# A two-layer encoder with expert retrieval: U ring of seven slots, V split at column 1024

## The reference

```python
def peer_ffn(xn, w_query, sub_keys, u, v):
    b, s, d = xn.shape
    K = PEER_TOPK
    q = (xn @ w_query).reshape(b, s, PEER_HEADS, 2, PEER_DKEY // 2)
    sc = jnp.einsum('bshpc,hpnc->bshpn', q, sub_keys).astype(jnp.float32)
    s_top, i_top = lax.top_k(sc, K)
    ...
    best, pos = lax.top_k(cand, K)
    expert = jnp.take_along_axis(cand_idx, pos, axis=-1)
    gate = jax.nn.softmax(best, axis=-1).astype(xn.dtype)
    ...
        act = jax.nn.gelu(jnp.einsum('tkd,td->tk', u[e], xt), approximate=False)
        return jnp.einsum('tk,tkd->td', g * act, v[e])
```

## Time and profile before

| what | us |
|---|---|
| median of 3 runs | 3390.19 (3378.97 to 3415.09) |
| the profiled execution | 3391.91, its span 3390.0 |
| DVE busy | 2366.2 (70%) |
| PE busy | 1921.9 (57%) |
| POOL busy | 1631.4 (48%) |
| data moved | 1067.07 MB, 315 GB/s over the span |

### The profile page before, as it was taken

One profiled execution on the slowest core, in us unless ns is written; L12 is line 12 of the kernel. 1 busy time (PEld: TensorE's weight loads), 2 busy tenths in 40 slices (PEclk: granted clock), 3 DMA queues, 4 the chain that ended last, 5 costly groups with the idle time before them and its releaser, 6 DMA issues.

```text
span 3390.0 us, 19864 instructions
## 1 busy us (share of the span) xinstructions
PE 1921.9 (57%) x6432; PEld 1415.5 (42%) x6432; DVE 2366.2 (70%) x3291; ACT 525.3 (15%) x1373; POOL 1631.4 (48%) x1028
## 2 busy tenths in 40 slices
PE   8999994714003300599999366322024105899992
PEld 4684543613003300467777245311023004677772
DVE  1340217889888887966666759889888889756668
ACT  1331200000009900100000000000079201000000
POOL 0000003355568877454444413546688878744445
PEclk9999997967555555589999688766555555799996
DMA  5334256787789999789999957877899998899998
GB/s 215 132 117 149 75 203 267 305 307 297 293 322 385 388 363 362 246 305 409 410 410 409 390 217 303 313 293 298 310 368 391 394 384 279 292 410 410 409 409 352
DMA packets 194502, 1067.07 MB, mean 315 GB/s; under 512 B 21856, under 2 KB 22240, under 8 KB 121312
## 3 DMA queue, kind: packets, MB, share of 16 engines
q0 software_dynamic: 147456, 822.15, 63.3%
q1 hardware_dynamic: 46944, 243.67, 18.2%
HBM read 1063.63 MB, written 2.10 MB: 314 GB/s over the span
## 4 chain that ended last, share of the span: by engine, by line
DMA 35%; DVE 21%; POOL 21%; PE 16%; issue 6%; ACT 0%; DVEq 0%; SPq 0%; POOLq 0%
DMA xnT<-pvg,idx_all 21%; POOL arena L392 16%; DMA arena<-pu,idx_all 13%; DVE arena L1012 8%; PE bank L1169 6%; DVE h L1031 3%; PE bank L1254 3%; POOL xnT L405 3%; POOL arena L405 3%; PE bank L1363 2%; PE bank L1410 1%; PE bank L1374 1%; DVE gB L1046 1%; PE bank L1432 1%; DVE gB L1042 1%
## 5 line engine op out<-in xcount | busy, mean ns | idle before, releaser
L392 POOL DMA_INDIRECT arena<-pu,idx_all x512 | 1056.0, 2063 | 1197.5 <-DVE idx_all L992 608.2
L1012 DVE CUSTOM_DVE_ANT_0 arena<-arena 128x2048 f32<-128x2048 f32 x512 | 1168.3, 2291 | 242.0 <-DMA arena<-pu,idx_all 239.3
L1459 PE MATMUL bank<-arena 128*128 128x480 f32 x2048 | 829.9, 569 | 2.0 <-ACT arena L651 1.4
L1459 PEld LDWEIGHTS bank<-arena 128*128 128x128 f32 x2048 | 605.0, 296 | 226.1 <-issue 4.9
L1031 DVE SCALAR_TENSOR_TENSOR h<-arena,cst,h 128x1088 f32<-128x1088 f32 x290 | 391.2, 1351 | 178.1 <-DMA arena<-pvg,idx_all 177.9
L405 POOL DMA_INDIRECT arena<-pvg,idx_all x290 | 313.9, 1082 | 305.8 <-DVE h L1031 271.7
L1031 DVE SCALAR_TENSOR_TENSOR h<-xnT,cst,h 128x1088 f32<-128x1088 f32 x222 | 299.7, 1351 | 140.9 <-DMA xnT<-pvg,idx_all 140.7
L405 POOL DMA_INDIRECT xnT<-pvg,idx_all x222 | 261.3, 1177 | 234.4 <-DVE h L1031 212.1
L1440 PE MATMUL bank<-cst,arena 128*128 128x128 f32 x8 | 2.8, 447 | 629.0 <-DVE cst L1018 629.0
L1440 PEld LDWEIGHTS bank<-cst,arena 128*128 128x128 f32 x8 | 1.2, 204 | 630.2 <-DVE cst L1018 630.2
L1410 PE MATMUL bank<-xnT,arena 128*128 128x256 f32 (+1 forms) x1280 | 244.7, 356 | 16.9 <-DMA arena<-wq 13.3
(11 more groups left out here) (193 smaller groups left out, 1630.8 us busy)
## 6 DMA issues: line engine op xcount, KB each, us to landing
arena<-pvd SPq DMA_DIRECT2D x256, 480.0 KB, 6.8
arena<-w_proj SPq DMA_DIRECT2D x22, 2048.0 KB, 8.2
arena<-wq SPq DMA_DIRECT2D x16, 2048.0 KB, 12.2
arena<-w_out SPq DMA_DIRECT2D x9, 2048.0 KB, 8.3
arena<-pu,idx_all POOLq DMA_INDIRECT x512, 7.8
gB<-gains SPq DMA_DIRECT2D x5, 1024.0 KB, 10.2
arena<-pvg,idx_all POOLq DMA_INDIRECT x290, 13.4
arena<-pool_w SPq DMA_DIRECT2D x1, 4096.0 KB, 14.3
```

Of the source, the lines that this page charges most:

```text
L392: nc.gpsimd.indirect_dma_start(U[:, n % UR], None, pu[L], bass.IndirectOffsetOnAxis(idx_all[:, g, k:k + 1], 0)).then_inc(u_got[n % UR], 16)
L1012: vec.tensor_tensor_reduce(out=u, in0=u, in1=xns[t], scale=1.0, scalar=0.0, op0=ALU.mult, op1=ALU.add, accum_out=act[:, t, hk:hk + 1]).the ...
L1459: ins = mm(psum[2 * t + c][:, 0:VH], W[t][:, :, n], vdense[:, n % DR, c * VH:(c + 1) * VH], start=n == 0, stop=n == NK - 1)
```

## The change

The U ring has seven slots in place of four. Slots 0 to 3 stay, the fifth is 2048 columns behind the one-hot tiles (arena 37248, over the third output weight slice of layer 0), the sixth and seventh depend on the block: for block 0 they lie at 12288 (over another output weight slice), for block 1 at 24576, over the keys and the routing scratch. Gathers 0 to 3 of layer 0 now wait for the first output projection, gathers 4 to 6 for all eight; gather 128 also waits until scores and expert numbers of all heads are done; every later gather waits for the dot seven before it, in place of four. V is split at column 1024: 1024 columns gathered (before 1088) and 1024 in the dense product (before 960, so matmuls of 512 columns in place of 480). The V ring has eight slots of 1024 in place of seven of 1088, four of them in xnT; the dense ring starts at 4096. Dots still read both operands from SBUF.

```diff
--- before.py
+++ after.py
@@ -52,17 +52,17 @@
 HALF = KC // 2
 
 WR = 3
-UR = 4
-VD, VG = 960, D - 960
+UR = 7
+VD, VG = 1024, D - 1024
 VH = VD // 2
-VR, DR = 7, 4
+VR, DR = 8, 4
 HK = PH * PK
 GROUPS = TB * PH
 ROWS = GROUPS * PK
 EVENTS = PH + 2
 QT = 4
 QUADS = P // QT
-W_AT, V_AT, VD_AT, T_AT = 8192, 0, 4352, 40960
+W_AT, V_AT, VD_AT, T_AT = 8192, 0, 4096, 40960
 POOLW = (2, 4, 8, 16)
 ARENA = 41344
 OUT_AT = 33152
@@ -116,7 +116,6 @@
             return carve
 
 
-        U = carver(0, ARENA)(UR, D)
         W = [carver(W_AT + t * P * P, ARENA)(P, P) for t in range(TB)]
         wqb2 = carver(W_AT, ARENA)(KC, 2 * P)
         wqb = carver(W_AT + 2 * KC * P * 2, ARENA)(2, KC, 2 * P)
@@ -135,6 +134,14 @@
         xn1 = carve(D)
         oh1 = carve(2, QT, P)
         oh2 = carve(2, QT, P)
+        fifth = carve(D)
+
+        def ring(at, n):
+
+            return [arena[:, at + i * D:at + (i + 1) * D] for i in range(n)]
+
+        shared = ring(0, 4) + [fifth]
+        U = [shared + ring(W_AT + KC * S, 2), shared + ring(W_AT + P * P, 2)]
         sT = carver(T_AT, ARENA)(3, P)
         wq_slots = [wqb[:, 0], wqb[:, 1], wqb2]
         xns = [xn0, xn1]
@@ -158,13 +165,13 @@
         exs, exr = spare(TB), spare(TB)
 
         xnT_flat = xnT[:, :, :].rearrange("p k s -> p (k s)")
-        vslots = [xnT_flat[:, i * VG:(i + 1) * VG] for i in range(3)]
-        vslots += [arena[:, V_AT + i * VG:V_AT + (i + 1) * VG] for i in range(VR - 3)]
+        vslots = [xnT_flat[:, i * VG:(i + 1) * VG] for i in range(4)]
+        vslots += [arena[:, V_AT + i * VG:V_AT + (i + 1) * VG] for i in range(VR - 4)]
         vdense = carver(VD_AT, W_AT)(DR, VD)
         goh1 = gB[:, 0:2 * QT * P].rearrange("p (b i n) -> p b i n", b=2, i=QT)
         goh2 = gB[:, 2 * QT * P:4 * QT * P].rearrange("p (b i n) -> p b i n", b=2, i=QT)
 
-        poolw = U.rearrange("p a b -> p (a b)").rearrange("p (g k c) -> p g k c", g=4, k=4)
+        poolw = carver(0, W_AT)(4, 4, BANK)
         slot1 = wqb[:, 1].rearrange("p k c -> p (k c)")
         PM = slot1[:, 0:D].rearrange("p (g t s) -> p g t s", g=4, t=TB)
         lsB = slot1[:, D:2 * D]
@@ -386,11 +393,17 @@
                 if n >= UR:
                     pool.wait_ge(s["dot_done"], L * ROWS + n - UR + 1)
                 elif L:
-                    pool.wait_ge(s["py_mm"], 4 + n + 1)
+                    pool.wait_ge(s["py_mm"], 4 + min(n, 3) + 1)
+                else:
+                    pool.wait_ge(s["out_mm"], TB * NO if n >= 4 else 1)
+                if n == HK:
+
+                    pool.wait_ge(s["sc_done"], (L + 1) * EVENTS)
+                    pool.wait_ge(s["idx_ready"], (L + 1) * EVENTS)
                 if k == 0:
                     pool.wait_ge(s["idx_ready"], L * EVENTS + event(g // PH, g % PH) + 1)
                 nc.gpsimd.indirect_dma_start(
-                    U[:, n % UR], None, pu[L], bass.IndirectOffsetOnAxis(idx_all[:, g, k:k + 1], 0)
+                    U[n // HK][n % UR], None, pu[L], bass.IndirectOffsetOnAxis(idx_all[:, g, k:k + 1], 0)
                 ).then_inc(u_got[n % UR], 16)
 
             def gather_v(L, m):
@@ -398,7 +411,7 @@
                 t, hk = m % TB, m // TB
                 if m >= VR:
                     pool.wait_ge(s["vacc_done"], L * ROWS + m - VR + 1)
-                elif m >= 3:
+                elif m >= 4:
                     pool.wait_ge(s["dot_done"], (L + 1) * ROWS)
                 else:
                     pool.wait_ge(s["q_mm"], (L + 1) * EVENTS)
@@ -1004,11 +1017,14 @@
                                        ex[:, tsl], exr[:, tsl].unsqueeze(2).to_broadcast([P, nt, PK]), ALU.mult))
 
 
+            ucount = [0] * UR
+
             def dot(L, n):
 
                 t, hk = n // HK, n % HK
-                v.wait_ge(u_got[n % UR], L * 16 * ROWS // UR + landed(n, UR))
-                u = U[:, n % UR]
+                ucount[n % UR] += 1
+                v.wait_ge(u_got[n % UR], 16 * ucount[n % UR])
+                u = U[t][n % UR]
                 vec.tensor_tensor_reduce(out=u, in0=u, in1=xns[t], scale=1.0, scalar=0.0, op0=ALU.mult, op1=ALU.add,
                                          accum_out=act[:, t, hk:hk + 1]).then_inc(s["dot_done"], 1)
 
```

## The result

The changed kernel takes 3215.3 us (median of 4, 3214.4 to 3215.6) against 3397.2 us (median of 4, 3379.0 to 3415.1) of the kernel before, run beside it: ratio 0.946, 95% interval 0.941 to 0.952. The profiled execution took 3215.5 us, 176.4 us less than that of before; the forecast was 187 less.

A forecast was written before the change was run, and what follows sets the result against it. The prediction held the four U slots, not bandwidth, for the bound of the 150 dots behind routing. Layer terms of -98 and -89 us took the profiled 3391.9 us to 3205 us; range 3168 to 3290, its terms' own ends 3176 and 3278.

The forecast's parts named there:

- The main step: 150 dots behind routing: four slots, not bandwidth, bind; 2.84 us a dot falls to 2.48 if the queue never runs dry.
- (b): Stage of 150 dots with nothing else on DVE, 946 to 1371 us in layer 0: forecast -60 and -46 us.
- six rows landed ahead: At dot 106, start of (b): six rows counted as landed, so 144 more must land; 365 us at 2.52 us each.
- (a): Stage of 74 dots beside routing, 668 to 946 us in layer 0: waits fall to 5 us, -34 and -30 us.
- Start of layer 0: First 32 dots: gathers 4 to 6 wait for all eight output projections, dot 4 starts near 551 us; +4 us.
- Layer 1: Start of layer 1: gathers 0 to 6 go at once, taking 5 of 8.1 us of waits off; -5 us.
- V: V split at 1024: shorter adds and gathers, dense matmuls 443 us with some ten adds behind; -8 us a layer.
- (c) and (d): One-hot tiles with V adds, then dense matmuls with the tail of adds: together -8 us a layer, from -10 to 0.
- The sum: Layer 0 -98 us, layer 1 -89 us: 3391.9 - 187 = 3205 us; forecast as summed given chance 0.70.
- Full DMA engines: First rival: transfers already full in (b), so a longer queue gains nothing there; 3311 us, chance 0.11.
- PE at the end: Second rival: PE sets the end of the dense part, +23 us a layer instead of -8; 3267 us, chance 0.13.
- POOL shut out by dots: Third rival: a full ring of seven blocks POOL's gathers, 3.33 us a dot in (b); 3539 us, chance 0.04.

The follow-up runs named there:

- the half dots with seven slots: The changed kernel, but each dot covers only the first 1024 of the 2048 columns, gathers staying whole: 3097.4 us (one run).
- routing three dots earlier: Changed kernel with layer 0's first slot order and V-add waits mended, plus each head's three routing pieces three dots earlier: 3187.6 us, ratio 0.938 to the kernel before.
- the ring alone: The kernel before with only the U ring raised to seven slots, V still split at 960: 3231.5 us, ratio 0.952.
- the half dots with four slots: U ring of four, V split at 1024, each dot over 1024 columns only, same bytes gathered: 3159.7 us (one run).
- the V part alone: The kernel before with only V split at 1024 and a V ring of eight, U ring of four: 3381.8 us, ratio 0.996.
- the half gathers: The changed kernel, but each U gather brings only 1024 columns while dots still run over 2048: 3144.8 us (one run).

## Why the prediction was right

**The main step held.** In (b) the four-slot ring and not the bandwidth was the bound, and with seven slots the landings follow each other at 2.5 us. Forecast -60 and -46 us, measured -55.8 and -42.7. It was reckoned from one paced run of three dots; the half dots with seven slots (367.2 us) and with four (371.9 us) show both halves of the claim.

**What was mis-sized in it** was "six rows landed ahead". Five rows lay ready at dot 106 (the gathers 106 to 110), number 111 landed 0.3 us into the stage, and number 112 could not be issued before 918.5 us. Its row landed at 926.3 us, 8.0 us into the stage; the other 143 followed at 2.51 us each, 359.4 us; with the last dot of 2.3 us that is the 369.7 us measured. The tempo of 2.52 us was right to 0.01; the start of the stage was 4 to 5 us short. Number 111 was late for want of a slot: dot 104 freed it at 911.1 us. What the wait of number 112 for its indices cost is not shown: without it, routing three dots earlier, (b) took as long.

**(a)** was forecast at -34 and -30 us and measured at -32.2 and -27.4. The 5 us of waits left there were found (5.3 and 6.1 us), but the reason given, the 2 MB weight slices, is only half of it. In layer 0, 3.9 of the 5.3 us stand at dots 35 to 37:

```profile
661.66 2.89 POOL L405 DMA_INDIRECT arena<-pu,idx_all  x1 [17.77 <-DVE idx_all L1005]
...
672.46 0.33 SPq L313 DMA_DIRECT2D arena<-wq  x1
...
680.93 2.29 DVE L1028 CUSTOM_DVE_ANT_0 arena<-arena 128x2048 f32<-128x2048 f32 x1 [1.70 <-DMA arena<-pu,idx_all]
...
685.26 2.29 DVE L1028 CUSTOM_DVE_ANT_0 arena<-arena 128x2048 f32<-128x2048 f32 x1 [2.03 <-DMA arena<-pu,idx_all]
```

The slice landed 12.6 us after its issue. Rows 35 and 36 landed 5.6 and 4.3 us behind the row before them where 2.5 is the tempo, 5.0 us too late together, which is the time of one slice. It could hurt because few rows lay ready: gather 32, the first row above, had stood 17.8 us for its indices, a wait that the kernel before does not have. Dots 51 and 53 wait the other 1.3 us, behind another slice (issued at 723.3 us) and behind gather 48, which stood 4.4 us for its indices. How much each of the two causes took was not measured. POOL waited for indices 4 times in the trace of before and 16 times in that after. Of these waits the prediction says only that the new one at gather 128 costs nothing, which is true; the old one at each head's first gather, late only at gathers 0 and 16 with four slots, became late at every head with seven.

**Start of layer 0.** Forecast +4, measured +3.3 (140.1 against 136.8 us; the ring alone, with the same start, took 137.7, so one execution tells it to some 2 us). Dot 4 began 23.2 us behind dot 0, where 12.3 us were before. The first row behind the pause took 10.3 us and not 7.85, as the 2 MB slice issued at 545.05 went with it, and dots 5 to 7 followed at 2.48; dot 7 was 6 us late, within the 2 to 7 forecast. Layer 1: forecast -5, measured -5.6.

**V.** Forecast -8 us a layer for (c) and (d), measured -9.2 and -9.3. The matmuls took 442.8 us against the 443 forecast by proportion, 0.865 us each, and 9 adds began behind them, 10 in layer 1, against ten.

**The sum.** -98 and -89 were forecast. Measured from the first dot of layer 0 to the end of its adds: 1396.5 us before, 1302.8 after, -93.7; in layer 1 1374.4 and 1289.7, -84.7. What is left over, 2 us, is shifts outside these stages. Of the missing 11 us, 7 to 8 are the starts of (b) and 4 are (a); V and the starts of the layers gave 4 more than forecast. The ends of the range were added up 1 to 2 us off: the terms named give 3178 (3174 with V's good end of -10) and 3276, not 3176 and 3278, which changes nothing.

**The rivals.** Full DMA engines: refuted by the half dots with four slots. The rule under it, that HBM binds at about 358 GB/s ("DMA: Bandwidth & Descriptors", Where 436 GB/s comes from, in the Trainium skill), does not hold for this program, which runs on one core: 421 GB/s over 340 us of gathers from HBM. PE at the end: refuted by the V part alone. POOL shut out by dots: refuted by the half gathers; by V adds: true at the start of the dense part, and worth 5 us a layer. "SBUF — State Buffer", SBUF: two separate sides, in the Trainium skill, says that the loser of the port waits for the whole instruction, and that a DVE instruction with two SBUF inputs takes it only against a GpSimd instruction that reads SBUF. That agrees with gathers that end 0.8 to 0.9 us behind an add or a dot, as a gather takes its row numbers from idx_all; that it is this read which is held up was not tried. The page speaks of one instruction. The prediction called the 8.12 us an agreement too, but they cover six adds, and the 8.9 us here cover eight: a gather was held over several instructions, which the page doesn't tell of.

## What to carry to other kernels

Read the bound of a ring from its tempo: where nearly every consumer waits for its row and these waits stand further apart on the mean than in the best paced run, the slots are too few, whatever the DMA share says. Here one slot more was nearly enough where the consumer runs on, and two more still paid a little where it pauses. A deeper ring asks earlier for everything that a transfer needs, so look at which producer (here the indices) is next in line. But a wait that is gone need not have cost anything: here ten of them went, and at most 1.6 us a layer with them, while the longest was left standing. A pause of the consumer is worth most where its rows are late anyway.

## What the runs showed of the hardware that was not expected

- A DMA share of 0.96 to 0.97 at 366 to 377 GB/s still had 10 to 13% to give: with more gathers queued the same stages ran at 414 and 415 GB/s, and at 421 GB/s and a share of 1.01 behind their first 30 us.
- Back-to-back V adds (scalar_tensor_tensor, 1.22 us apart) held one gather of POOL over eight instructions, 8.9 us; dots, each followed by a read of the accumulator, let it in every time (no U gather took over 3.1 us), though they too stood without a gap (2.21 us apart). An add that waits for its predecessor lets it in as well (2.2 us at most). Whether it is the gap or the accumulator read that lets POOL in was not tried.
- With the four-slot ring and whole dots the time was uneven: 3367 to 3411 us for the kernel before in 13 runs, 3357 to 3411 for the V part alone in 10, and (b) of the latter took 430.1 us in layer 0 and 400.6 in layer 1 of one execution. With seven slots the sets of four and six runs lie within 1.2 to 7.5 us.
